# A hybrid decoder step with a paged cache: the order of two gathers in one slot of the decode's ring

## The reference

```python
k_past = cache_k[l, page_table].reshape(bs, past, N_HEADS, 2, QK_HEAD)   # bs 8, past 8192
v_past = cache_v[l, page_table].reshape(bs, past, N_HEADS, V_HEAD)
k_all = jnp.concatenate([k_past.astype(k.dtype), k], axis=1)
v_all = jnp.concatenate([v_past.astype(v.dtype), v], axis=1)
o = diff_attend(q, q_pos_s, k_all, v_all, k_pos_s, lam)

def diff_attend(q, q_pos, k, v, k_pos, lam):
    s = jnp.einsum('bqhcd,bkhcd->bhcqk', q, k) * (QK_HEAD ** -0.5)
    s = jnp.where(k_pos[None, :] <= q_pos[:, None], s, -jnp.inf)
    p = jax.nn.softmax(s, axis=-1)
    a = p[:, :, 0] - lam * p[:, :, 1]
    return jnp.einsum('bhqk,bkhd->bqhd', a, v)
```

## Time and profile before

| | |
|---|---|
| median of 3 runs | 2301.07 us (2290.49 to 2301.31) |
| profiled execution, time | 2304.27 us |
| its span | 2302.5 us |
| TensorE busy | 1839.8 us, 80% of the span |
| VectorE busy | 1056.6 us, 46% |
| ScalarE busy | 489.0 us, 21% |
| Pool busy | 319.1 us, 14% |
| gathers of keys on Pool | 128, 120.6 us busy |
| gathers of values on Pool | 128, 120.7 us busy |
| mean over the span | 176 GB/s |

### The profile page before, as it was taken

The page is one execution under the profiler, slowest core; times in us unless marked ns, Lnnn a source line. Parts: engine busy times, 40 slices in busy tenths (PEclk is TensorE's granted clock), DMA queues, the critical chain, the costliest instruction groups (busy, mean ns, idle before and its releaser), DMA issues.

```text
span 2302.5 us, 40476 instructions
## 1 busy us (share of the span) xinstructions
PE 1839.8 (80%) x17492; PEld 1481.2 (64%) x17492; DVE 1056.6 (46%) x1532; ACT 489.0 (21%) x831; POOL 319.1 (14%) x287
## 2 busy tenths in 40 slices
PE   4799999556665765766765966999999997999992
PEld 1378899444554554554544965777777776888881
DVE  2324121577776685776734564111121112465547
ACT  0210111012212212122122031121211212333331
POOL 0000000123242332422321017000000000000003
PEclk7799999687797987988877987999999998999996
DMA  9701132677898988989975110121212214311102
GB/s 312 265 30 43 37 109 92 232 288 300 334 410 321 418 330 327 414 330 396 363 311 224 37 37 19 55 91 55 73 55 69 77 55 173 106 42 38 37 28 94
DMA packets 133284, 404.41 MB, mean 176 GB/s; under 512 B 12153, under 2 KB 76665, under 8 KB 100338
## 3 DMA queue, kind: packets, MB, share of 16 engines
q0 software_dynamic: 37392, 270.55, 29.1%
q1 hardware_dynamic: 87426, 127.52, 16.4%
q10 hardware_dynamic: 8320, 4.19, 0.7%
HBM read 377.79 MB, written 24.51 MB: 175 GB/s over the span
## 4 chain that ended last, share of the span: by engine, by line
PE 65%; DVE 17%; DMA 11%; issue 5%; ACT 1%; DVEq 0%; POOL 0%; SPq 0%; ACTq 0%
PE psum L745 27%; PE psum L994 12%; PE psum L753 10%; DVE k_turned L1429 6%; DMA k_ring<-cache_k,page_idx 6%; DMA ada_w<-w_ada 3%; PE psum L844 2%; PE psum L854 2%; PE psum L1001 2%; DVE p_t L426 2%; PE psum L728 2%; PE psum L824 1%; DVE x_lo L1274 1%; DMA v_ring<-cache_v,page_idx 1%; DVE soft L1380 1%
## 5 line engine op out<-in xcount | busy, mean ns | idle before, releaser
L1429 DVE STREAM_TRANSPOSE k_turned<-k_ring 128x2048 f32<-128x2048 f32 x128 | 295.4, 2308 | 5.3 <-DMA k_ring<-cache_k,page_idx 5.1
L745 PE MATMUL psum<-x_hi,w_hi 128*128 128x512 f32 x896 | 282.0, 396 | 0.0
L745 PE MATMUL psum<-x_lo,w_hi 128*128 128x512 f32 x896 | 277.9, 392 | 0.0
L844 PE MATMUL psum<-k_turned,q_blocks 128*32 128x128 f32 x4096 | 157.0, 300 | 151.0 <-DVE k_turned L1429 150.7
L745 PE MATMUL psum<-x_hi,w_lo 128*128 128x512 f32 x896 | 276.9, 390 | 0.0
L1293 DVE TENSOR_TENSOR w_lo<-w_raw,w_hi 128x2048 fp32r<-128x2048 f32 x37 | 86.9, 2350 | 364.1 <-ACT w_hi L1049 354.4
L844 PEld LDWEIGHTS psum<-k_turned,q_blocks 128*32 128x32 f32 x4096 | 117.0, 119 | 204.6 <-issue 152.9
L994 PE MATMUL psum<-d_hi,h_hi 128*128 128x256 f32 x704 | 209.1, 297 | 12.3 <-DVE d_lo L1643 10.7
L994 PE MATMUL psum<-d_lo,h_hi 128*128 128x256 f32 x704 | 199.8, 284 | 0.0
L994 PE MATMUL psum<-d_hi,h_lo 128*128 128x256 f32 x704 | 199.4, 283 | 0.0
L745 PEld LDWEIGHTS psum<-x_hi,w_hi 128*128 128x128 f32 x896 | 166.3, 189 | 45.0 <-ACT h_out L1185 4.5
(11 more groups left out here) (228 smaller groups left out, 2548.1 us busy)
## 6 DMA issues: line engine op xcount, KB each, us to landing
ada_w<-w_ada SPq DMA_DIRECT2D x12, 2048.0 KB, 9.2
w_raw<-w_in SPq DMA_DIRECT2D x12, 1024.0 KB, 5.3
w_raw<-w_gate SPq DMA_DIRECT2D x11, 1024.0 KB, 5.3
w_raw<-w_up SPq DMA_DIRECT2D x11, 1024.0 KB, 6.2
h_store<-h_out SPq DMA_DIRECT2D x11, 1024.0 KB, 7.8
h_all<-h_store SPq DMA_DIRECT2D x11, 1024.0 KB, 5.7
d_raw<-w_down SPq DMA_DIRECT2D x44, 256.0 KB, 2.9
x_rows<-x_prompt SPq DMA_DIRECT2D x2, 2048.0 KB, 16.8
```

The costliest lines, as they stand in the source:

```text
L745: last = mm(psum[:, 2 * ft + c, 0:CH], w[:, s, k, ft * P:(ft + 1) * P], x[:, k, c * CH:(c + 1) * CH], start=k == 0 and j == 0, stop=k == K ...
L844: last = mm(psum[QUAD * h:QUAD * (h + 1), g % 2, 0:GP * QUAD], q_blocks[:, h, d, :], k_turned[:, g % 2, :, h * HD + d * QUAD:h * HD + (d + ...
L1429: v.transpose(k_turned[:, g % 2].rearrange("p j n -> p (j n)"), k_ring[:, g].rearrange("p j n -> p (j n)")).then_inc(k_free, 1)
```

## The change

Inside a slot of the ring the two calls of `gather` change places. The arguments, the waits and the number of DMAs remain; pass 0 still has only keys and pass 8 only values.

```diff
@@ load_pages @@
             for b in range(B + 1):
                 for r in range(REVS):
                     for g in range(RING):
+                        if b:
+                            gather(v_pages, v_ring, v_in, v_free, b - 1, r, g)
                         if b < B:
                             gather(k_pages, k_ring, k_in, k_free, b, r, g)
-                        if b:
-                            gather(v_pages, v_ring, v_in, v_free, b - 1, r, g)
```

## The result

| | before | changed |
|---|---|---|
| median | 2300.24 us (2290.49 to 2301.31, 4 runs) | 2336.92 us (2330.38 to 2343.27, 4 runs) |
| profiled execution, its span | 2304.27, 2302.5 us | 2337.28, 2335.5 us |

The ratio is 1.0169, with a 95% interval from 1.0129 to 1.0208: the change makes the kernel 36 us slower in the medians and 33.0 us between the two profiled executions. The forecast was 2336.

What follows compares the result with a forecast made beforehand. The decode was taken as bound by the gathers queued between the restart and the last key landing. Two lost transfers, 5.02 us in each of 7 sequences, sum to 35.1 us on 2301.07, giving 2336 us, range 2318 to 2351.

Steps and rivals of the forecast that it cites:

- all seven sequences: Decode, sequences 1 to 7: each bound by how many gathers pass between queue's restart and last key gather's landing.
- The small slack: VectorE slightly late behind the last key landing (0.6 us in sequence 6): takes perhaps 1 us off the sum.
- step 1: Queue's restart behind the softmax: 3.80 us later, losing one transfer, 2.51 us for each sequence.
- step 2: End of each sequence: last value gather passes ahead of the last key gather, one more transfer, 2.51 us.
- step 3: Within rounds: key gathers go out 2 to 4 us later, covered by at least 1.8 us, so costed at nothing.
- A: Restart and last transposes: one of the two lost places is recovered, 17.6 us slower, 2319; chance 0.11.
- B: Ring within rounds: fewer gathers outstanding, it runs dry, bubbles add 14 us to the 35, 2350; chance 0.12.
- thin ring: Follow-up rival, all slots: key and value slots reissued late together, bubbles add up; 0 to 2 us for one swapped slot.
- C: Last pass: values come earlier where TensorE waits for them, up to 27 us gone, 2274 or 2309; chance 0.03.
- D: Queue: DMA engines share gathers instead of taking them in order, so no change, 2301 to 2306; chance 0.04.

Runs made afterwards that it cites:

- halved pair: Kernel before and changed kernel, each gather moving half a row (0.5 MiB): 2293.23 us keys first, 2297.41 us values first.
- slot (3,3) alone: Kernel before with values ahead only in slot 3 of round 3, the last before the softmax: 2325.63 against 2300.30 us, ratio 1.0109.
- experiment 3: Kernel before with values ahead in every slot but slot 0 of round 1 and slot 3 of round 3: 2320.64 against 2300.30 us.
- experiment 7: Kernel before with values ahead in eleven of sixteen slots, keys first in slots 0, 1, 3 of round 1 and slot 3 of rounds 2, 3: 2311.03 us.
- (2,3) alone, experiment 5: Kernel before with values ahead only in slot 3 of round 2: 2324.11 against 2298.81 us, ratio 1.0106.
- experiment 6: Kernel with values ahead only in slot 3 of round 2, plus eight idle matmuls ahead of that slot's key group: 2317.36 us, 1.0095 against the kernel before.
- experiment 4: Kernel before with values ahead only in slot 0 of round 1 and slot 3 of round 3: 2340.89 against 2300.30 us, ratio 1.0170.
- experiment 1: Kernel before with values ahead only in slot 0 of round 1, the first behind a softmax: 2318.88 against 2300.30 us, ratio 1.0081.

## Why the prediction was right, point by point

**What bounds the decode.** Right about the queue, but too simple, and wrong for "all seven sequences". The queue is full (399 GB/s over the whole stretch, 401 before), it serves in order, and v(3,3) and k(3,3) land 2.5 us apart. But in the kernel before VectorE stood idle for k(3,3) in sequences 1, 3 and 7 only, 0.3 to 0.5 us, and for k(2,3) in sequences 2, 3, 4, 5 and 7; in sequence 6 the last transpose has no idle time ahead of it. What I took for one bound with a slack below 1 us is several: the place of k(3,3), and the places of the keys before it with the computing behind them. The small slack that I read and then left aside as worth 1 us was the sign of that. The halved pair shows it: with no key late any more, k(3,3) is turned only 1.45 us earlier.

**The restart (step 1).** Right in place and size. v(1,0) is issued at 736.59, 6.22 us behind the first transpose, as before (727.55 - 721.16 = 6.39); nothing goes ahead of it. Alone it costs 18.6 us, forecast 17.6.

**The tail (step 2).** Right in place, short in size: 25 us alone where the step had 17.6. The term left out is TensorE's clock: the slower groups behind the last transpose are 1.85 us in each softmax, 11 us in six. That idle matmuls would win this back was tried at slot (2,3) and not here. In the whole change the term doesn't come on top: the last column of the table is 26.52 against 26.72. There the gap in front of the last key group isn't longer than before, at most 1.9 us in both kernels, where it is 2.2 to 4.2 us with slot (3,3) alone, and the last key group takes the long time in sequence 3 only, before and after.

**Within rounds (step 3).** Wrong. I costed the inner slots at nothing because the ring had cover. The cover held: in experiments 3 and 7 k(3,3) lands as long behind v(1,0)'s issue as before. But a swapped inner slot also moves a key one place back, and this costs even where k(3,3) keeps its place: 20 us for fourteen slots, 24 for (2,3) alone (of these perhaps 7 for the clock, by experiment 6), 12 for eleven. From the transpose of k(2,3) to that of k(3,3) it was 67.09 - 46.76 = 20.3 us before the change, and in the four sequences in which k(3,3) wasn't waited for, so that this is computing, 20.3 to 21.1; eight places are 20.1.

**The sum.** 7 x 5.02 = 35.1 was forecast, 33.6 is read, and 36 is the difference of the medians. It came out right although step 3 was wrong because the bounds run side by side: the whole change moves k(2,3) and k(3,3) by two places each, so the path through either gives the same 5 us, and the inner slots' cost is the same delay seen earlier, not another. That the sum fits is in this part luck: the prediction had no reason for it. Had the change been in fourteen slots, the same reasoning would have said 0 to 6 us and been off by 14 to 20.

**Two terms inside the sum were off against each other.** I took 7.8 us for v(1,0)'s own landing. But 7.8 is the least of the landings that the trace has, and not one into an empty queue. In the changed kernel v(1,0) lands 5.9 us after its issue in sequence 3, with nothing ahead of it (5.5 to 5.9 in five sequences, 7.1 and 7.7 in two); then the first seven places take 2.76 us each (to k(1,3), issued at 747.20 and landed at 761.74) and the other sixteen 2.51. So 5.9 + 19.3 + 40.2 = 65.3 us comes close to 7.8 + 23 x 2.51 = 65.5, also by luck. The Trainium skill (DMA: Bandwidth & Descriptors, "Anatomy of one DMA") has 4.4 us by its formula, an estimate; the trace lies above it, but nearer than I had put it. On the rate the trace again disagrees with the HBM limit that the Trainium skill gives (DMA: Bandwidth & Descriptors, "Where 436 GB/s comes from"): places at the end are 2.5 us apart, not 2.93.

**The rivals.** Half of it (A, 2319) is refuted by the result and by experiment 4. A ring that runs dry (B) is refuted by the landings: k(3,3) lands 65.0 to 65.5 us behind v(1,0)'s issue in all seven sequences of the changed kernel, and in experiments 3 and 7 as before; the thin ring as the main cause falls with the halved pair and with experiments 1 and 4, where one or two slots cost 19 and 39 us. Faster in the last pass (C): the chain there waits 9.64, 7.69 and 8.80 us for values, 26.1 in all, against 26.7, so it is unchanged. Sharing instead of order (D): the landings refute it.

## What to carry to other kernels

When a full queue feeds a chain, count places: what a reordered transfer costs is the number of transfers put ahead of the one that is waited for last, times the service time, once for each refill of the queue, and a transfer that used to run in the dry gap counts as one. But do this for each transfer on which some computing hangs, not for the last alone; where transfers and computing are nearly equally long, the delays run side by side and are neither additive nor zero. And look at what the waiting engine does with its idle time: a TensorE that is left idle for a late operand may come back at half its clock, and then a late operand costs more than its lateness.

## What the runs showed of the hardware that I had not expected

- TensorE's granted clock can fall over short waits. After 4.27 us idle it was 0.61 over the next 7 us, after 0.76 us idle 1.00. 32 matmuls take 1.93 or 1.94 us at the low level and 1.08 at the high one. But the last wait alone doesn't tell which: in the changed kernel the last key group takes 1.94 us behind 1.88 us idle in sequence 3 (first line) and 1.08 behind 1.86 in sequence 5 (second), and in experiment 5 one takes 1.08 behind 3.78.

```profile
804.45 1.94 PE L844 MATMUL psum<-k_turned,q_blocks 128*32 128x128 f32 x32 [1.88 <-DVE k_turned L1429]
...
1004.67 1.08 PE L844 MATMUL psum<-k_turned,q_blocks 128*32 128x128 f32 x32 [1.86 <-DVE k_turned L1429]
```

- In the softmax 5.86 us of idle matmuls brought the granted clock to 1.00, and after 5 us more, of which the engine was busy for 1.51, it was at 0.51 again.
- An indirect gather of 1 MiB behind a softmax, with no other gather ahead of it, lands 5.5 to 7.7 us after its issue in the changed kernel, and a full queue delivers one each 2.5 us.
- Gathers of half rows are less efficient: from 560 to 1180 us they take 0.59 of the DMA engines' time for 189 GB/s, where the kernel before takes 0.90 for 363.
